# Six experts written out without a loop, and a reordered entry to the delta rule's triangular inverse

## The chip, the core and the metric

The kernel runs on one core of a Trainium2 chip: TensorE (matrix products, PE in the profile), VectorE (DVE), ScalarE (ACT), GpSimd (POOL) and SyncE (SP), which here issues the weight transfers. The engines run their own instruction streams and wait for each other on semaphores. The time is that of one execution on the device in microseconds, and the median over runs is what counts.

## The reference

The model is a trunk of two layers over 256 tokens of width 1024. The even layer adds a window attention with 8 heads (64 wide) and a gated delta rule with 4 heads (128 wide), followed by a dense SwiGLU. The odd layer is a Mamba-2 mixer, followed by a top-2-of-8 mixture of SwiGLU experts, 1024 by 3584 each. Each sub-layer ends in a layer norm of ALPHA * x + f(x). The two parts that the change touches are, in short:

```
# gated delta rule, per chunk and head
gc = cumsum(g);  decay = exp(gc_i - gc_j) below the diagonal
A  = strict_lower((beta k) k^T * decay);   attn = (q k^T) * decay
u, w = solve(I + A, [beta v, beta k exp(gc)])
v_new = u - w S;  o = (q exp(gc)) S + attn v_new
S = S exp(gc_last) + (k exp(gc_last - gc))^T v_new
# experts, all eight on the tokens that chose them
out += combine[:, e] * (silu(x Wg[e]) * (x Wu[e])) Wd[e]
```

## The kernel before

All weights come from HBM as fp32 in pieces of 1 MB into a ring of raw buffers. ScalarE rounds each piece into a high part (w_hi, L698 and L951), VectorE subtracts to get the low part (w_lo, L1127 and L1575), and TensorE multiplies three times: high by high, high by low, low by high (in the experts L2366 to L2368). Nothing schedules the work: each engine's stream stands in the source in the order in which it runs, with waits on semaphores that are written by hand. PSUM is one tensor `ps` of eight banks of 128x512 fp32. The delta rule's tiles all lie in one SBUF tensor, so the profile calls them "arena"; here they are told apart by their lines.

**Entry to the delta rule.** The 256 tokens make two row tiles t = 0, 1, and each row tile is one chunk of 128 for the four heads. TensorE runs the projections; the last is that of the attention's queries, `halves(N_Q, ...)`, in two halves, with `running_sums` between them (L1928, L1929): the running sums of g, into bank 3. VectorE, after the low part of the projection's last piece (L1127), normalises k and q (L1210, L1212), copies the attention's k and v (L1216), negates the running sums (L1218, L1219), copies the attention's queries (L1223) and applies the rotary tables. TensorE then spreads the running sums and beta over rows (L1943 to L1948) and forms the products k k^T and k q^T (`kk_products`, L1937 and L1938). ScalarE makes the decays (L760). VectorE multiplies products and decays into attnT (L1250) and AT (L1251, L1252). Then TensorE turns k and v (L1958), VectorE scales them into kdec, vb and kbe (L1256 to L1262), and the inverse starts.

**The inverse** has seven levels (LEVELS) for both row tiles. `level(lv)` masks AT into LT (L1271); TensorE multiplies LT by X (L2050); ScalarE copies the result (L796); TensorE multiplies by XT (L2060, L2061); VectorE subtracts (L1352, L1354 in level 0, L1357, L1359 later). Between the levels stand pieces of the window attention: `turn_qk` transposes its queries (L1969) and its key (L1973), VectorE copies them (L1279, L1281), and so on. The queries' transposes wait for the scalings of k and v (semaphore kv_scaled), since they reuse banks.

**The experts.** Expert 0 starts outside the loop. A loop `Fori(0, E - 2, 2)` on TensorE, ScalarE, VectorE and SyncE then runs three passes, each of which finishes expert i, runs expert i + 1 and begins expert i + 2 (`expert_rest`, `expert_head`); experts 6 and 7 end outside. Inside the loop the counts waited for are computed in registers. Near the end of each expert's steady part TensorE turns the next expert's tokens, eight transposes (L2362).

Of the kernel before, what the change touches and what calls it, by code (L numbers as in the profile page):

```python
# [35 lines left out]
P = 128  # L36
# [26 lines left out]
E = 8  # L63
# [112 lines left out]
def build(nc, dram, out, limit=99):  # L176
    with ExitStack() as ctx:
# [297 lines left out]
        def _(sp):  # L475
# [110 lines left out]
            with sp.Fori(0, E - 2, 2) as i:  # L586
                link_loads(i, (i, 0), i + 1)
                steady_loads(i + 1, (i, 1))
                link_loads(i + 1, (i, 1), i + 2)
                steady_loads(i + 2, (i, 2))  # L590
# [85 lines left out]
        def _(act):  # L676
# [80 lines left out]
            for t in range(TT):  # L757
                act.wait_ge(sem("dn_gcrow"), t + 1)
                for h in range(DH):
                    act.activation(decT[:, t * DH + h, :], ps[:, t, h * P:(h + 1) * P], ACT.Exp, bias=ngc[:, t, h:h + 1]  # L760
                                   ).then_inc(sem("dn_dec"), 1)

# [300 lines left out]
            with act.Fori(0, E - 2, 2) as i:  # L1063
                expert_rest((i, 0), 0, (i, 1), False, i + 1)
                expert_head((i, 1), 1, (i, 0), i)
                expert_rest((i, 1), 1, (i, 2), False, i + 2)
                expert_head((i, 2), 0, (i, 1), i + 1)
# [27 lines left out]
        def _(dve):  # L1095
# [109 lines left out]

            n = N0 - 1
            dense_low(n, n % RAW_D, n % CUT)
            rn3 = rn[:, :].rearrange("p (k t) -> p k t", t=SEQ)
# [4 lines left out]

            dve.wait_ge(d_piece_used, CUT + N_KV + 2)
            for t in range(TT):
                dve.tensor_copy(qkv[:, t, 512:768], ps[:, 4 + t, 0:256]).then_inc(sem("kv_copied"), 1)  # L1216
            dve.wait_ge(sem("dn_gc"), 1)
            link(TS(ngc[:, :, :], ps[:, 3, 0:TT * DH].rearrange("p (t h) -> p t h", t=TT), -1.0, None, ALU.mult))  # L1218
            TTO(ddk[:, :], ps[:, 3, 8:12], ngc[:, 0, :], ALU.add).then_inc(sem("dn_cols"), 1)  # L1219
# [25 lines left out]

            for t in range(TT):
                dve.wait_ge(sem("dn_dec"), DH * (t + 1))
                dve.wait_ge(sem("dn_kk"), t + 1)
                hs = slice(t * DH, (t + 1) * DH)
                TTO(attnT[:, hs, :], four(ps[:, 6 + t, :]), decT[:, hs, :], ALU.mult)  # L1250
                link(TTO(AT[:, hs, :], four(ps[:, 4 + t, :]), decT[:, hs, :], ALU.mult))  # L1251
                TTO(AT[:, hs, :], AT[:, hs, :], four(ps[:, 2 + t, :]), ALU.mult).then_inc(sem("dn_A"), 1)  # L1252
            dve.wait_ge(sem("dn_A"), TT)

            dve.wait_ge(sem("kv_turned"), 1)
            TTO(kdec[:, :, :], four(ps[:, 4, :]), bc(dke[:, :], P), ALU.mult)  # L1256
            dve.wait_ge(sem("kv_turned"), 2)
            TTO(vb[:, 0:4, :], four(ps[:, 5, :]), bc(beta[:, 0, :], P), ALU.mult)
            dve.wait_ge(sem("kv_turned"), 3)
            TTO(kbe[:, :, :], four(ps[:, 6, :]), bc(bege[:, :], P), ALU.mult)  # L1260
            dve.wait_ge(sem("kv_turned"), 4)
            TTO(vb[:, 4:8, :], four(ps[:, 7, :]), bc(beta[:, 1, :], P), ALU.mult).then_inc(sem("kv_scaled"), 1)  # L1262
# [82 lines left out]
            level(1)  # L1345
            for lv in range(LEVELS):
# [14 lines left out]
                if lv == 0:  # L1361
                    dve.wait_ge(sem("inv_X"), 2)
                if lv + 2 < LEVELS:
                    level(lv + 2)
# [378 lines left out]
            with dve.Fori(0, E - 2, 2) as i:  # L1743
                expert_rest((i, 0), 0, (i, 1), i, None, rank)
                expert_head((i, 1), 1, None, None)
                expert_rest((i, 1), 1, (i, 2), i + 1, None, rank)
                expert_head((i, 2), 0, None, None)
# [59 lines left out]
        def _(pe):  # L1807
# [115 lines left out]
            def running_sums():  # L1923
                pe.wait_ge(sem("dn_gb"), 1)
                pe.wait_ge(sem("norm_ln"), 4)
                pe.wait_ge(sem("ln_loaded"), 16 * 3)
                g8 = gdn[:, :, :].rearrange("p t h -> p (t h)")
                mm(ps[:, 3, 0:8], tri, g8, start=True, stop=True)  # L1928
                mm(ps[:, 3, 8:12], ones[:, :], gdn[:, 0, :], start=True, stop=True).then_inc(sem("dn_gc"), 1)  # L1929
# [11 lines left out]
            pe.wait_ge(sem("dn_cols"), 1)  # L1941
            for t in range(TT):
# [6 lines left out]
            pe.wait_ge(sem("dn_qk"), 2)  # L1949
            for t in range(TT):  # L1950
                pe.wait_ge(sem("q_copied"), t + 1)
                pe.wait_ge(sem("kv_copied"), t + 1)
                kk_products(t)
            pe.wait_ge(sem("dn_A"), TT)
            for t in range(TT):
                for w_ in range(2):
                    for h in range(DH):
                        last = pe.transpose(ps[:, 4 + 2 * t + w_, h * P:(h + 1) * P], dnT[:, 4 + 4 * w_ + h, t * P:(t + 1) * P], ident)  # L1958
                    last.then_inc(sem("kv_turned"), 1)

# [82 lines left out]
            for lv in range(LEVELS):  # L2043
                for t in range(TT):
# [6 lines left out]
                    last.then_inc(sem("inv_P"), 1)  # L2051
                attention(lv, 0)
# [434 lines left out]
            with pe.Fori(0, E - 2, 2) as i:  # L2487
# [43 lines left out]
```

## Time and profile before

| what | value |
|---|---|
| median of 3 runs | 1596.58 us (1596.31 to 1596.8) |
| profiled execution | 1595.24 us |
| its span, first to last instruction | 1593.4 us |
| TensorE busy | 1559.8 us, 98% |
| VectorE busy | 1280.6 us, 80% |
| ScalarE busy | 970.1 us, 61% |
| granted TensorE clock, mean | 0.996 of full speed |
| chain that ended last | TensorE 92%, VectorE 5% |

The profile is of one execution. Its span is measured from the first to the last instruction, and 1.84 us of the execution's time lie around it. Busy time is the sum of an engine's instructions; a share near 100% says that the time can fall only where that engine waits, or by giving it less to do. The chain that ended last is followed back from the last instruction to whatever released each step, so it shows what the end of the program hung on.

### The profile page before, as it was taken

What the parts mean: (1) busy time and instruction counts of PE and PEld (TensorE: products, weight loads), DVE (VectorE), ACT (ScalarE), POOL (GpSimd) and SP (SyncE); (2) the same over time, 40 slices, a digit from 0 to 9 for tenths busy, and PEclk for the clock granted to TensorE, in tenths of its full rate; (3) what the DMA queues carried; (4) which work ended last, traced back from release to release, by engine and by line L of the source; (5) the groups of instructions that cost most, each with busy time, mean ns of one, the idle gap of its engine ahead of it and who ended that gap; (6) DMA issues with size and microseconds to landing.
All of it is one profiled execution on the core that took longest, in us unless ns stands there. A gap on an engine that the chain in (4) does not pass through costs nothing.

```text
span 1593.4 us, 22120 instructions
## 1 busy us (share of the span) xinstructions
PE 1559.8 (98%) x8609; PEld 1324.1 (83%) x8609; DVE 1280.6 (80%) x1060; ACT 970.1 (61%) x822; POOL 55.1 (3%) x43
## 2 busy tenths in 40 slices
PE   9989999999999999999999999999999999999996
PEld 7878599997999787888888878888878888888885
DVE  6777645447777797999889889889889888888997
ACT  4414244443553644777777777777777777777773
POOL 4000000002000000020000000000000000000100
PEclk9999999999999999999999999999999999999998
DMA  9250365554557118999999999999999999999992
GB/s 323 70 196 1 114 203 184 184 185 156 179 177 261 62 35 307 360 399 395 394 394 383 387 378 363 389 380 377 384 379 370 383 374 378 392 372 389 394 397 79
DMA packets 221760, 459.40 MB, mean 288 GB/s; under 512 B 7685, under 2 KB 64737, under 8 KB 221665
## 3 DMA queue, kind: packets, MB, share of 16 engines
q1 hardware_dynamic: 215488, 441.76, 76.4%
q10 hardware_dynamic: 4464, 11.60, 2.0%
q0 software_dynamic: 1712, 4.68, 0.8%
q8 instruction: 70, 1.15, 0.3%
q14 instruction: 26, 0.21, 0.0%
HBM read 444.38 MB, written 13.63 MB: 287 GB/s over the span
## 4 chain that ended last, share of the span: by engine, by line
PE 92%; DVE 5%; ACT 1%; issue 1%; POOL 0%; DMA 0%; DVEq 0%; ACTq 0%
PE ps L2366 19%; PE ps L2368 19%; PE ps L2367 19%; PE ps L1849 6%; PE ps L1851 6%; PE ps L1850 6%; PE ps L1842 2%; PE ps L2391 2%; PE ps L2130 1%; PE ps L2131 1%; PE ps L2132 1%; PE ps L2291 1%; PE ps L2293 1%; PE ps L2292 1%; PE ps L2060 1%
## 5 line engine op out<-in xcount | busy, mean ns | idle before, releaser
L1575 DVE TENSOR_TENSOR w_lo<-raw,w_hi 128x2048 fp32r<-128x2048 f32 x252 | 576.8, 2291 | 69.2 <-ACT w_hi L951 68.3
L951 ACT CAST w_hi<-raw 128x2048 fp32r<-128x2048 f32 x252 | 482.8, 1916 | 129.2 <-PE ps L2368 129.2
L2366 PE MATMUL ps<-w_hi,xg_hi 128*128 128x512 f32 x672 | 267.7, 398 | 3.1 <-issue 2.3
L2368 PE MATMUL ps<-w_hi,xg_lo 128*128 128x512 f32 x672 | 262.4, 391 | 0.0
L2367 PE MATMUL ps<-w_lo,xg_hi 128*128 128x512 f32 x672 | 261.6, 389 | 0.0
L698 ACT CAST w_hi<-raw 128x2048 fp32r<-128x2048 f32 (+1 forms) x72 | 135.6, 1883 | 182.1 <-PE ps L1851 133.6
L1127 DVE TENSOR_TENSOR w_lo<-raw,w_hi 128x2048 fp32r<-128x2048 f32 (+1 forms) x71 | 167.7, 2367 | 94.7 <-ACT w_hi L698 94.7
L1849 PE MATMUL ps<-xT_hi,w_hi 128*128 128x256 f32 x768 | 218.1, 284 | 0.3 <-DVE xT_lo L1120 0.3
L1851 PE MATMUL ps<-xT_hi,w_lo 128*128 128x256 f32 x768 | 217.4, 283 | 0.0
L1850 PE MATMUL ps<-xT_lo,w_hi 128*128 128x256 f32 x768 | 217.4, 283 | 0.0
L1575 DVE TENSOR_TENSOR xT_lo<-raw,xT_hi 128x2048 fp32r<-128x2048 f32 x84 | 192.3, 2290 | 29.9 <-ACT xT_hi L951 29.9
L951 ACT CAST xT_hi<-raw 128x2048 fp32r<-128x2048 f32 x84 | 160.9, 1915 | 43.8 <-PE ps L2368 43.8
L2366 PEld LDWEIGHTS ps<-w_hi,xg_hi 128*128 128x128 f32 x672 | 126.3, 188 | 28.8 <-issue 4.0
L1849 PEld LDWEIGHTS ps<-xT_hi,w_hi 128*128 128x128 f32 x768 | 147.4, 192 | 1.7 <-DVE xT_lo L1120 1.3
L2368 PEld LDWEIGHTS ps<-w_hi,xg_lo 128*128 128x128 f32 x672 | 126.2, 188 | 27.2
L1850 PEld LDWEIGHTS ps<-xT_lo,w_hi 128*128 128x128 f32 x768 | 147.4, 192 | 0.3
L1851 PEld LDWEIGHTS ps<-xT_hi,w_lo 128*128 128x128 f32 x768 | 147.4, 192 | 0.0
L2367 PEld LDWEIGHTS ps<-w_lo,xg_hi 128*128 128x128 f32 x672 | 126.5, 188 | 24.6
L2366 PE MATMUL ps<-w_hi,ehT_hi 128*128 128x512 f32 x336 | 131.5, 391 | 0.0
L2367 PE MATMUL ps<-w_lo,ehT_hi 128*128 128x512 f32 x336 | 130.8, 389 | 0.0
L2368 PE MATMUL ps<-w_hi,ehT_lo 128*128 128x512 f32 x336 | 130.8, 389 | 0.0
L2368 PE MATMUL ps<-xT_hi,xg_lo 128*128 128x512 f32 x224 | 87.3, 390 | 0.0
(398 smaller groups left out, 2164.4 us busy)
## 6 DMA issues: line engine op xcount, KB each, us to landing
raw<-in_moe_w_gate SPq DMA_DIRECT2D x112, 1024.0 KB, 7.8
raw<-in_moe_w_up SPq DMA_DIRECT2D x112, 1024.0 KB, 8.4
raw<-in_moe_w_down SPq DMA_DIRECT2D x112, 1024.0 KB, 8.4
raw<-in_ssm_w_in SPq DMA_DIRECT2D x20, 1024.0 KB, 5.3
raw<-in_ffn_w_gate SPq DMA_DIRECT2D x11, 1024.0 KB, 5.3
raw<-in_ffn_w_up SPq DMA_DIRECT2D x11, 1024.0 KB, 5.3
raw<-in_ffn_w_down SPq DMA_DIRECT2D x11, 1024.0 KB, 4.9
raw<-in_even_w_in SPq DMA_DIRECT2D x10, 1024.0 KB, 12.9
```

The source lines that it names most:

```text
L698: act.copy(w_hi[:, c, 0:size], raw[:, i, 0:size]).then_inc(sem("dense_hi_made"), 1)
L951: act.copy(e_hi((n + 2 * odd) % CUT_E), raw[:, i, :]).then_inc(sem("hi_made"), 1)
L1127: TTO(w_lo[:, c, 0:size], raw[:, i, 0:size], w_hi[:, c, 0:size].bitcast(F32), ALU.subtract).then_inc(d_lo_made, 1)
L1575: TTO(e_lo(c), raw[:, n % RAW, :], e_hi(c).bitcast(F32), ALU.subtract).then_inc(lo_made, 1)
L1842: last = mm(ps[:, 4 + 2 * t + n, :], mixT[:, k, t * P:(t + 1) * P], w[:, kk, 512 * n:512 * n + 512], start=k == 0, stop=k == KD - 1)
L1849: mm(out_ap, whi, xT_hi[:, k, :], start=first, stop=False)
L1850: mm(out_ap, whi, xT_lo[:, k, :], start=False, stop=False)
L1851: return mm(out_ap, wlo, xT_hi[:, k, :], start=False, stop=last_)
L2366: mm(out_ap, hi, whi, start=start, stop=False)
L2367: mm(out_ap, hi, wlo, start=False, stop=False)
L2368: return mm(out_ap, lo, whi, start=False, stop=stop)
L2391: last = pe.transpose(ps[:, 4, c * P:(c + 1) * P], eh[:, side(j), c * P:(c + 1) * P], ident)
```

## The change

It has two parts that share no code.

First, the loop over pairs of experts becomes a Python loop on all four engines (the diff shows the line on ScalarE; SyncE, VectorE and TensorE have the same), which writes experts 1 to 6 out as straight code with constant counts. The order of the work inside is the same.

Second, the entry to the delta rule's inverse:
- The running sums go to bank 4 behind the attention's k and v (columns 256 to 267), and so wait for the copies of k and v in place of the logarithms of the norms. VectorE makes those copies ahead of the last low part, and negates the sums right behind it.
- TensorE interleaves the two row tiles: rows and products of tile 0, then of tile 1.
- attnT of tile 1 is made after level 0's masks (`made_attn`), and level 1's masks after level 0's differences.
- The transposes of k and v run by row tile (`turn_kv`): tile 0 ahead of the inverse, tile 1 behind level 0's product.
- ScalarE, in place of VectorE, scales them: 16 activations with a scale per partition, behind the decays.

```diff
-            with act.Fori(0, E - 2, 2) as i:
+            for i in range(0, E - 2, 2):
...
+            act.wait_ge(sem("dn_dke"), 2)
+            act.wait_ge(sem("dn_gb"), 1)
+            for i, (dst, by) in enumerate(((kdec[:, :, :], dke[:, :]), (vb[:, 0:4, :], beta[:, 0, :]),
+                                           (kbe[:, :, :], bege[:, :]), (vb[:, 4:8, :], beta[:, 1, :]))):
+                act.wait_ge(sem("kv_turned"), i + 1)
+                bank = ps[:, (4, 6, 5, 7)[i], :]
+                for h in range(DH):
+                    last = act.activation(dst[:, h, :], bank[:, h * P:(h + 1) * P], ACT.Copy, scale=by[:, h:h + 1])
+            last.then_inc(sem("kv_scaled"), 1)
...
+            dve.wait_ge(d_piece_used, CUT + N_KV + 2)
+            for t in range(TT):
+                dve.tensor_copy(qkv[:, t, 512:768], ps[:, 4 + t, 0:256]).then_inc(sem("kv_copied"), 1)
             n = N0 - 1
             dense_low(n, n % RAW_D, n % CUT)
+            dve.wait_ge(sem("dn_gc"), 1)
+            link(TS(ngc[:, :, :], ps[:, 4, 256:264].rearrange("p (t h) -> p t h", t=TT), -1.0, None, ALU.mult))
+            TTO(ddk[:, :], ps[:, 4, 264:268], ngc[:, 0, :], ALU.add).then_inc(sem("dn_cols"), 1)
...
+            def made_attn(t):
+                hs = slice(t * DH, (t + 1) * DH)
+                return TTO(attnT[:, hs, :], four(ps[:, 6 + t, :]), decT[:, hs, :], ALU.mult)
...
-                TTO(attnT[:, hs, :], four(ps[:, 6 + t, :]), decT[:, hs, :], ALU.mult)
+                if t == 0:
+                    made_attn(0)
...
-            TTO(kdec[:, :, :], four(ps[:, 4, :]), bc(dke[:, :], P), ALU.mult)
...
             level(0)
-            level(1)
+            made_attn(1).then_inc(sem("dn_A"), 1)
...
                 if lv == 0:
                     dve.wait_ge(sem("inv_X"), 2)
+                    level(1)
...
                 pe.wait_ge(sem("dn_gb"), 1)
-                pe.wait_ge(sem("norm_ln"), 4)
                 pe.wait_ge(sem("ln_loaded"), 16 * 3)
+                pe.wait_ge(sem("kv_copied"), TT)
...
-            pe.wait_ge(sem("dn_qk"), 2)
-            for t in range(TT):
+                if t == 0:
+                    pe.wait_ge(sem("dn_qk"), 2)
                 pe.wait_ge(sem("q_copied"), t + 1)
                 pe.wait_ge(sem("kv_copied"), t + 1)
                 kk_products(t)
-            pe.wait_ge(sem("dn_A"), TT)
-            for t in range(TT):
+
+            def turn_kv(t):
+                pe.wait_ge(sem("dn_A"), (1, 3)[t])
                 for w_ in range(2):
                     for h in range(DH):
-                        last = pe.transpose(ps[:, 4 + 2 * t + w_, h * P:(h + 1) * P], dnT[:, 4 + 4 * w_ + h, t * P:(t + 1) * P], ident)
+                        last = pe.transpose(ps[:, 4 + t + 2 * w_, h * P:(h + 1) * P], dnT[:, 4 + 4 * w_ + h, t * P:(t + 1) * P], ident)
                     last.then_inc(sem("kv_turned"), 1)
+
+            turn_kv(0)
...
                     last.then_inc(sem("inv_P"), 1)
+                if lv == 0:
+                    turn_kv(1)
```

VectorE's rows from the first product with the decays on, before (L1250 attnT, L1251 and L1252 AT, L1256 to L1262 the scalings, L1271 masks, L1352 and L1354 the differences of level 0):

```order
L1250 TENSOR_TENSOR arena<-ps,arena 128x512
L1251 TENSOR_TENSOR arena<-ps,arena 128x512
L1252 TENSOR_TENSOR arena<-arena,ps 128x512
L1250 TENSOR_TENSOR arena<-ps,arena 128x512
L1251 TENSOR_TENSOR arena<-ps,arena 128x512
L1252 TENSOR_TENSOR arena<-arena,ps 128x512
L1256 TENSOR_TENSOR arena<-ps,arena 128x512
L1258 TENSOR_TENSOR arena<-ps,arena 128x512
L1260 TENSOR_TENSOR arena<-ps,arena 128x512
L1262 TENSOR_TENSOR arena<-ps,arena 128x512
L1271 TENSOR_TENSOR arena<-arena,const 128x512 x4
```

and in the changed kernel, whose lines are others (L1256 attnT, L1264 and L1265 AT, L1275 masks, L1356 and L1358 the differences):

```order
L1256 TENSOR_TENSOR arena<-ps,arena 128x512
L1264 TENSOR_TENSOR arena<-ps,arena 128x512
L1265 TENSOR_TENSOR arena<-arena,ps 128x512
L1264 TENSOR_TENSOR arena<-ps,arena 128x512
L1265 TENSOR_TENSOR arena<-arena,ps 128x512
L1275 TENSOR_TENSOR arena<-arena,const 128x512 x2
L1256 TENSOR_TENSOR arena<-ps,arena 128x512
L1356 TENSOR_TENSOR arena<-const,arena 128x512
L1358 TENSOR_TENSOR arena<-const,ps 128x512
L1356 TENSOR_TENSOR arena<-const,arena 128x512
L1358 TENSOR_TENSOR arena<-const,ps 128x512
L1275 TENSOR_TENSOR arena<-arena,const 128x512 x4
```

The four scalings are gone, attnT of tile 1 stands behind the first two masks, and level 1's masks stand with those of level 2 behind the differences.

TensorE's rows behind the key products, before, with the semaphores waited for (L1958 transposes of k and v, L2050 the inverse's products, L1969 transposes of the queries):

```order
L1958 MATMUL ps<-const,arena 128x128 [waits dn_A]
L1958 MATMUL ps<-const,arena 128x128 x15
L2050 MATMUL ps<-const,arena 128x128 [waits inv_L]
L2050 MATMUL ps<-const,arena 128x128 x3
L2050 MATMUL ps<-const,arena 128x128 [waits inv_L]
L2050 MATMUL ps<-const,arena 128x128 x3
L1969 MATMUL ps<-const,arena 128x128 [waits kv_scaled,rope_done]
L1969 MATMUL ps<-const,arena 128x128 x7
L2050 MATMUL ps<-arena 128x128 [waits inv_X,inv_L]
L2050 MATMUL ps<-arena 128x128 x3
L2050 MATMUL ps<-arena 128x128 [waits inv_X,inv_L]
```

and in the changed kernel (L1965, L2059 and L1978 in the same roles):

```order
L1965 MATMUL ps<-const,arena 128x128 [waits dn_A]
L1965 MATMUL ps<-const,arena 128x128 x7
L2059 MATMUL ps<-const,arena 128x128 [waits inv_L]
L2059 MATMUL ps<-const,arena 128x128 x3
L2059 MATMUL ps<-const,arena 128x128 [waits inv_L]
L2059 MATMUL ps<-const,arena 128x128 x3
L1965 MATMUL ps<-const,arena 128x128 [waits dn_A]
L1965 MATMUL ps<-const,arena 128x128 x7
L1978 MATMUL ps<-const,arena 128x128 [waits kv_scaled,rope_done]
L1978 MATMUL ps<-const,arena 128x128 x7
L2059 MATMUL ps<-arena 128x128 [waits inv_X,inv_L]
```

The sixteen transposes are split in two eights, the second of which stands between the inverse's first product and the queries.

TensorE's rows where the loop over pairs begins, before (L2487 is the loop, L2366 to L2368 an expert's three products):

```order
L2368 MATMUL ps<-xT_hi,ehT_lo 128x512
L2487 UNCONDITIONAL_BRANCH
L2487 ISA
L2378 ISA [waits e_h]
L2366 MATMUL ps<-w_hi,xg_hi 128x512 [waits lo_made]
L2367 MATMUL ps<-w_lo,xg_hi 128x512
L2368 MATMUL ps<-w_hi,xg_lo 128x512
```

and at the same place in the changed kernel, where the products are L2377 to L2379:

```order
L2379 MATMUL ps<-xT_hi,ehT_lo 128x512
L2377 MATMUL ps<-w_hi,xg_hi 128x512 [waits lo_made,e_h]
L2378 MATMUL ps<-w_lo,xg_hi 128x512
L2379 MATMUL ps<-w_hi,xg_lo 128x512
L2377 MATMUL ps<-w_hi,xg_hi 128x512
```

The branch and the two register instructions are gone, and the wait for e_h stands on the product itself.

## Rows read from the trace of the kernel before

**Rows 1.** The page: busy time, share of span, instructions; queue: packets, MB, share.
```profile
PE 1559.8 (98%) x8609; PEld 1324.1 (83%) x8609; DVE 1280.6 (80%) x1060; ACT 970.1 (61%) x822; POOL 55.1 (3%) x43
...
q8 instruction: 70, 1.15, 0.3%
```

**Rows 2.** Chain that ended last, experts: start us, us, what; issue is unexplained time.
```profile
852.76 0.87 PE ps L2362 x8
943.08 1.19 issue
972.74 0.88 PE ps L2362 x8
1091.22 0.87 PE ps L2362 x8
1181.54 1.07 issue
1211.06 0.87 PE ps L2362 x8
1329.54 0.87 PE ps L2362 x8
1448.02 0.87 PE ps L2362 x8
```

**Rows 3.** Busy us of PE, PEld, DVE, ACT, POOL; clock, DMA, GB/s by stretch.
```profile
90.00:99.00 9.00, 4.73 (x41) 4.31 (x40) 8.15 (x14) 0.00 (x0) 0.00 (x0) 1.00 1.10 352
700.00:940.00 240.00, 240.00 (x1095) 198.86 (x1095) 213.54 (x119) 178.55 (x121) 0.00 (x0) 1.00 1.03 389
1580.00:1593.00 13.00, 1.20 (x6) 0.64 (x4) 10.44 (x17) 0.00 (x0) 2.09 (x2) 0.63 0.22 84
```

**Rows 4.** Timeline of TensorE, delta rule's entry: start us, us, operation, [idle before].
```profile
76.48 0.36 PE L1928 MATMUL ps<-arena,const 128*128 128x8 f32 x2 [1.01 <-issue]
...
76.92 0.48 PE L1880 MATMUL ps<-w_hi,xT_hi 128*128 128x512 f32 x1
...
82.49 0.39 PE L1943 MATMUL ps<-maskb,identb 128*128 128x512 bf16 x1
...
89.85 0.39 PE L1938 MATMUL ps<-arena 128*128 128x128 f32 x2
92.57 1.96 PE L1958 MATMUL ps<-const,arena 128*128 128x128 f32 x16 [2.34 <-DVE arena L1252]
96.47 2.05 PE L2050 MATMUL ps<-const,arena 128*128 128x128 f32 x16 [1.94 <-DVE arena L1271]
98.36 1.04 PE L1969 MATMUL ps<-const,arena 128*128 128x128 f32 x8
99.57 2.33 PE L2050 MATMUL ps<-arena 128*128 128x128 f32 x16 [0.17 <-DVE arena L1354]
102.61 0.44 PE L1973 MATMUL ps<-const,arena 128*128 128x128 f32 x2 [0.71 <-DVE arena L1279]
```

**Rows 5.** Timeline of VectorE in the same stretch.
```profile
74.10 2.29 DVE L1127 TENSOR_TENSOR w_lo<-raw,w_hi 128x2048 fp32r<-128x2048 f32 x1 [0.99 <-ACT w_hi L698]
...
81.16 0.75 DVE L1216 COPY arena<-ps 128x256 f32<-128x256 f32 x2
...
88.59 0.69 DVE L1250 TENSOR_TENSOR arena<-ps,arena 128x512 f32<-128x512 f32 x1 [2.82 <-PE ps L1938]
...
93.33 0.69 DVE L1256 TENSOR_TENSOR arena<-ps,arena 128x512 f32<-128x512 f32 x1 [0.82 <-PE ps L1958]
...
95.74 2.49 DVE L1271 TENSOR_TENSOR arena<-arena,const 128x512 f32<-128x512 f32 x4
```

**Rows 6.** Timeline of ScalarE, logarithms, exponentials of decays, one attention exponential.
```profile
73.97 2.41 ACT L750 ACTIVATE arena<-ps,eps_rms 128x512 f32<-128x512 f32 x4
...
83.81 1.14 ACT L760 ACTIVATE arena<-ps,arena 128x128 f32<-128x128 f32 x4 [1.30 <-PE ps L1945]
...
127.89 0.39 ACT L771 ACTIVATE arena<-arena 128x128 f32<-128x128 f32 x1
```

More of the change, by code:

```diff
@@ L585, in _ @@
             steady_loads(0, (0, 0))
-            with sp.Fori(0, E - 2, 2) as i:
+            for i in range(0, E - 2, 2):
                 link_loads(i, (i, 0), i + 1)
@@ L1062, in _ @@
             act.wait_ge(sem("x_placed"), 16 * 2 * TT)
-            with act.Fori(0, E - 2, 2) as i:
+            for i in range(0, E - 2, 2):
                 expert_rest((i, 0), 0, (i, 1), False, i + 1)
@@ L1212, in _ @@
             TTO(dnT[:, 4:8, :], dnT[:, 4:8, :], rn3[:, 4:8, :], ALU.mult).then_inc(sem("dn_qk"), 1)
-            dve.wait_ge(d_piece_used, CUT + N_KV + 2)
-            for t in range(TT):
[L1216 to L1219, printed above, removed]
             dve.wait_ge(d_piece_used, CUT + N0)
@@ L1253, in _ @@
             dve.wait_ge(sem("dn_A"), TT)
-            dve.wait_ge(sem("kv_turned"), 1)
-            TTO(kdec[:, :, :], four(ps[:, 4, :]), bc(dke[:, :], P), ALU.mult)
[L1257 to L1262, printed above, removed]
             def level(lv):
@@ L1742, in _ @@
             expert_head((0, 0), 0, None, None, False, True)
-            with dve.Fori(0, E - 2, 2) as i:
+            for i in range(0, E - 2, 2):
                 expert_rest((i, 0), 0, (i, 1), i, None, rank)
@@ L1924, in running_sums @@
                 pe.wait_ge(sem("dn_gb"), 1)
-                pe.wait_ge(sem("norm_ln"), 4)
                 pe.wait_ge(sem("ln_loaded"), 16 * 3)
+                pe.wait_ge(sem("kv_copied"), TT)
                 g8 = gdn[:, :, :].rearrange("p t h -> p (t h)")
-                mm(ps[:, 3, 0:8], tri, g8, start=True, stop=True)
-                mm(ps[:, 3, 8:12], ones[:, :], gdn[:, 0, :], start=True, stop=True).then_inc(sem("dn_gc"), 1)
+                mm(ps[:, 4, 256:264], tri, g8, start=True, stop=True)
+                mm(ps[:, 4, 264:268], ones[:, :], gdn[:, 0, :], start=True, stop=True).then_inc(sem("dn_gc"), 1)
             pe.wait_ge(sem("dn_conv"), NDN // 2)
@@ L1941, in _ @@
             pe.wait_ge(sem("dn_cols"), 1)
+            pe.wait_ge(sem("norm_ln"), 4)
             for t in range(TT):
@@ L1953, in _ @@
                 kk_products(t)
-            pe.wait_ge(sem("dn_A"), TT)
-            for t in range(TT):
+            def turn_kv(t):
+                pe.wait_ge(sem("dn_A"), (1, 3)[t])
                 for w_ in range(2):
                     for h in range(DH):
-                        last = pe.transpose(ps[:, 4 + 2 * t + w_, h * P:(h + 1) * P], dnT[:, 4 + 4 * w_ + h, t * P:(t + 1) * P], ident)
+                        last = pe.transpose(ps[:, 4 + t + 2 * w_, h * P:(h + 1) * P], dnT[:, 4 + 4 * w_ + h, t * P:(t + 1) * P], ident)
                     last.then_inc(sem("kv_turned"), 1)
+            turn_kv(0)
             def turn_qk(n):
@@ L2486, in _ @@
             expert_head((0, 0), 0, None, 0)
-            with pe.Fori(0, E - 2, 2) as i:
+            for i in range(0, E - 2, 2):
                 expert_rest((i, 0), 0, (i, 1), False, True)
```

## The prediction

> **What bounds the kernel now.** I read the page first: TensorE is busy 98% of the span [rows 1]. So a change is worth what it takes out of TensorE's idle time, and nothing else. Then the chain of waits, to see where that idle time lies near the edits. In the experts the reader is to look for the eight-transpose rows of L2362, which come once per expert. From 972.74 to 1091.22 and from 1329.54 to 1448.02 they stand 118.48 us apart, but from 852.76 to 972.74 it is 119.98 and from 1091.22 to 1211.06 it is 119.84 [rows 2]. In each of the two long stretches lies one "issue" row (1.19 and 1.07 us), time in which TensorE waited for nothing that the profile shows, and each is where the loop over pairs jumps back. There are three passes, so two jumps. The way out of the loop, which is no jump, lies between 1329.54 and 1448.02 and costs nothing. Inside a pass TensorE is never idle: 240.00 of 240 us [rows 3].
>
> Last the timelines of the delta rule. TensorE stands still four times: 1.01 us before the running sums, 2.34 before the k and v transposes (L1958), 1.94 before the inverse's first products (L2050), 0.71 before L1973 [rows 4]. The last three wait for VectorE, which works there without a pause. So around 88 to 102 us VectorE's queue sets the end.
>
> **The experts written out.** It removes the two jumps back on TensorE, and those of ScalarE, VectorE and SyncE, whose own delay at the same places lies behind TensorE's. What goes is (119.98 - 118.48) + (119.84 - 118.48) = 1.50 + 1.36 = 2.86 us. If only the visible idle time goes, it is 1.19 + 1.07 = 2.26; I take 2.86, since the straight stretches show the whole period without a jump. Arithmetic on registers goes too, at no gain, since the periods inside a pass already have TensorE full. SyncE's transfers keep their order and their waits. What is added is code that is read once instead of a body read three times; the trace of before shows no written-out run of experts 1 to 6, so the lower bound is a loss, priced below as a rival.
>
> A rule of the Trainium skill bears on this (Runtime: NRT & Kernel Launch, section "Instruction fetch mechanics"): code is fetched ahead in sequence only, and a taken branch to a page that isn't held stalls the engine. By that rule both jumps go and the sum stays 2.86. The same section says that crossing a block is "mostly hidden", which leaves open what the written-out code pays; that is the rival.
>
> **The delta rule's entry, step by step**, with times on the clock of the trace of before.
>
> 1. The running sums no longer wait for the logarithms (L750, which end at 73.97 + 2.41 = 76.38 [rows 6]). They run at 75.47, right behind the first half of the queries' projection. But its second half also needs the low part of its weights, which VectorE makes from 74.10 to 76.39 [rows 5]. So it starts at about 76.47 in place of 76.92: 0.45 us, not 1.01. The two copies of k and v (0.75 us) now stand ahead of that low part; VectorE was idle 0.99 us there, so they are covered with 0.24 to spare. Were they not, the whole chain would slip by what is missing.
> 2. From 82.49 TensorE runs back to back for 7.58 us, until 89.85 + 0.22 [rows 4]; the edit only interleaves the two row tiles. It now starts at 82.04, tile 0 is done after half of it, at 85.83, tile 1 at 89.62. VectorE's three products of a tile take 1.97 us (88.59 to 92.52, two tiles [rows 4, 5]). Those of tile 0 are now hidden under TensorE's tile 1. Behind tile 1 stand two products in place of three, about 1.4 us: done at 91.15 in place of 92.52.
> 3. The four scalings (from 93.33 to 95.74, 2.41 us) leave VectorE, and level 1's mask goes behind. So level 0's two masks (0.6 us each, from four in 2.4) run from 91.2, and the inverse's first product starts at 92.0 in place of 96.47. It takes 1.89 us for both tiles, to 93.9. The second half of the k and v transposes (eight, 0.9 us) follows to 94.8; the first half ran at 89.6 to 90.5, while TensorE waited anyway.
> 4. A new wait: the query transposes need all four scalings, now on ScalarE. It was idle there, with nothing queued behind but the copies of the next level. The trace has no such scaling. The nearest row is four exponentials of the same 128x128 tiles from PSUM: 1.14 us [rows 6]. The first two sets run at 90.2 to 92.5, hidden. The last two can start at 94.4 and take 2.28, to 96.7. From above, one by one at 0.39, which one activation of this size takes alone [rows 6], they take 3.12, 0.8 us later. From below, at no cost, the wait vanishes and level 1's mask (96.2) becomes the late one, 1.4 us better. I take 1.14 a set, the same tile shape.
> 5. The query transposes start at 96.8 (before 98.36), 0.9 us for two tiles. Level 1's product starts at 97.7 (99.57). By then VectorE has finished four differences (93.0 to 95.5) and four masks (to 98.0), and copies the first turned tile by 98.7. So level 1's product ends at 99.6 and the key transpose follows at once, where it was waiting for that copy until 102.61. It takes 0.22, not the 0.44 after a wait. The next products begin at 99.85 in place of 103.05.
>
> That is 3.2 us on the path (2.4 to 4.6 by the bounds of step 4). Behind it every engine has the same order as before, and nothing waits for a fixed time: each later start shifts alike.
>
> **Sum.** 2.86 + 3.2 = 6.1 us. The profiled execution took 1595.24 us (span 1593.4 and 1.84 around it), which gives 1589.1. The median of the runs, 1596.58, lies 1.34 above the profiled one; on its scale the forecast is 1590.5.
>
> **Rivals.**
> - *Only the experts gain.* The scalings' wait takes the place of the removed one: the query transposes start as late as before and 3.2 us stay. For this the last two scalings would have to take more than twice 2.28 us and hold back the pass up to the key transpose. The idle ScalarE and the exponentials' row speak against it. Time 1596.6 - 2.9 = 1593.7.
> - *Only the delta rule gains.* Two or three new stalls of the jump's size in the written-out code eat the 2.86. Time 1596.6 - 3.2 = 1593.4.
> - *Slower: TensorE runs out of code.* The larger instruction queue moved 70 packets; TensorE has 8609 matmul records [rows 1], each with a weight load (a pass shows 1095 and 1095 in 240 us [rows 3]), so 246 records a packet. A pass is nine packets; three passes are 27 places where the next packet could come late behind weight transfers, which move 389 GB/s there. A late one costs what a jump does, 1.13 us on average. From six such stalls the gain is gone; if one place in three stalls, the time is 1590.5 + 9 x 1.13 = 1600.7. Against it: the loop's passes, longer than anything else in the experts, show 240.00 us of work in 240. That packet count fits all executed records, so the body seems to be read anew in each pass already, without a stall within. The rule named above, with crossings mostly hidden, says the same.
> - *Neither shows.* 1596.6. A clock that fell in the delta rule would do this: the granted clock was 0.63 of 2.4 GHz in the last 13 us, between its two levels, after TensorE had nearly stopped (1.20 us of work). But with 4.73 us of work in the 9 us from 90 it stayed at 1.00 [rows 3], and the new order leaves shorter pauses, about 1.5 and 2.0 us.
>
> **How the numbers follow.** Forecast 0.72, only experts 0.08, only delta rule 0.10, neither 0.04, slower 0.06. The likeliest case alone spans 4.7 (2.26 + 2.4) to 7.5 (2.86 + 4.6): 1589.1 to 1591.9. The two half cases end at 1593.7, so the range that should hold 8 in 10 is 1589.0 to 1593.8. A measurement of this kernel can tell about 0.2% (3.2 us) from no change. Only-delta sits on that line and is split: faster 0.72 + 0.05 = 0.77, same 0.08 + 0.05 + 0.04 = 0.17, slower 0.06.
>
> **What would show it.** Right: all L2362 periods 118.48, and no "issue" row between them; the second half of the queries' projection at 76.5; the inverse's first product at 92.0, about 4.5 earlier; the query transposes released by ScalarE at about 96.8 after a pause of some 2 us; and everything from the key products to the output projection 3.2 earlier. Wrong: issue gaps of TensorE inside an expert, a lower granted clock after 90 us, VectorE's low part later than 76.4, or a pause of TensorE later in the inverse that was not there before.

## The result, and the profile after

| | before | changed |
|---|---|---|
| median of 6 runs, us | 1596.69 (1595.88 to 1597.97) | 1589.75 (1588.71 to 1591.40) |
| profiled execution, us (span) | 1595.24 (1593.4) | 1589.78 (1588.0) |

The ratio is 0.9949 [0.9939, 0.9959]: 8.1 us faster [6.5, 9.7] on 1596.58, which makes 1588.4. That is 0.6 us below the lower edge of the forecast's range, and a gain 2.0 us larger than the 6.1 forecast. The ratio is not the quotient of the two medians in the table; that is 0.9957, or 6.9 us. The same kernel run again (`after_again`, below) gave 6.5 us by its ratio and 8.5 by its medians. So the gain is known only to within 6.5 to 8.5 us; all four figures lie above the 6.1 forecast, and the two smaller ones would have lain inside its range. The two profiled executions differ by 5.46 us, 0.6 less than forecast. So the trace shows less gain than the timed runs, and that gap is the thing to explain.

First the page of the changed kernel; these two rows answer to [rows 1].

```profile
PE 1557.5 (98%) x8608; PEld 1323.1 (83%) x8609; DVE 1277.9 (80%) x1056; ACT 975.7 (61%) x838; POOL 55.1 (3%) x43
...
q8 instruction: 64, 1.05, 0.3%
```

The chain that ended last, in the experts, as in [rows 2] (L2362 is now L2373): start us, us, what.

```profile
850.21 0.87 PE ps L2373 x8
968.69 0.87 PE ps L2373 x8
1087.17 0.88 PE ps L2373 x8
...
1205.65 0.87 PE ps L2373 x8
...
1442.61 0.87 PE ps L2373 x8
```

All periods are 118.48, and no "issue" row stands between. One window over all the experts (busy us of PE, PEld, DVE, ACT, POOL; clock, DMA, GB/s) answers to the 240 us of [rows 3]: TensorE has 920.00 us of work in 920.

```profile
640.00:1560.00 920.00, 920.00 (x4193) 762.22 (x4193) 824.54 (x473) 687.28 (x466) 17.70 (x8) 1.00 1.02 383
```

The timeline of TensorE in the delta rule's entry, which answers to [rows 4]:

```profile
75.53 0.29 PE L1933 MATMUL ps<-arena,const 128*128 128x8 f32 x2
...
76.66 0.50 PE L1885 MATMUL ps<-w_hi,xT_hi 128*128 128x512 f32 x1 [0.62 <-DVE w_lo L1136]
...
92.26 2.05 PE L2059 MATMUL ps<-const,arena 128*128 128x128 f32 x16 [1.43 <-DVE arena L1275]
...
97.11 1.06 PE L1978 MATMUL ps<-const,arena 128*128 128x128 f32 x8 [1.93 <-ACT arena L769]
98.01 1.95 PE L2059 MATMUL ps<-arena 128*128 128x128 f32 x16
99.80 0.38 PE L1982 MATMUL ps<-const,arena 128*128 128x128 f32 x2
100.02 0.39 PE L2071 MATMUL ps<-arena 128*128 128x128 f32 x2
```

The pauses that were 1.01, 2.34, 1.94 and 0.71 us are now 0.62, 1.43 and 1.93. The new wait is the one forecast, L1978 for ScalarE. ScalarE's two pairs of scalings (compare [rows 6]) take 2.18 us each, where 2.28 was taken from the exponentials:

```profile
90.52 2.18 ACT L769 ACTIVATE arena<-ps,arena 128x128 f32<-128x128 f32 x8 [2.06 <-PE ps L1965]
94.79 2.18 ACT L769 ACTIVATE arena<-ps,arena 128x128 f32<-128x128 f32 x8 [2.09 <-PE ps L1965]
```

Where the 5.46 us of the two traces came from is read off where the same instruction stands in both. At the start the changed kernel loses 0.21: its first product with weights starts at 11.19 in place of 10.98, in code that no edit touches. The first product behind the key transposes (L2071) is this one in the kernel before:

```profile
102.88 0.39 PE L2060 MATMUL ps<-arena 128*128 128x128 f32 x2
```

It now starts 2.87 earlier, so the entry gave 3.08. Mamba's output projection at about 575 us gives 0.3 back; the loop adds 2.86; 5.4 in all.

### The profile page after: what moved, and what is told of

Its sections match the earlier page's. It is cut to its first block, busy times and chain, and to the rows that moved or that the text cites. A ratio compares the mean times of both kernels' runs of the same rounds, so it can differ in the third digit from the quotient of the medians.

```text
span 1588.0 us, 20779 instructions
## 1 busy us (share of the span) xinstructions
PE 1557.5 (98%) x8608; PEld 1323.1 (83%) x8609; DVE 1277.9 (80%) x1056; ACT 975.7 (61%) x838; POOL 55.1 (3%) x43
## 4 chain that ended last, share of the span: by engine, by line
PE 92%; DVE 5%; ACT 1%; issue 1%; POOL 0%; DMA 0%; DVEq 0%; SPq 0%; ACTq 0%
PE ps L2377 19%; PE ps L2379 19%; PE ps L2378 19%; PE ps L1854 6%; PE ps L1856 6%; PE ps L1855 6%; PE ps L1847 2%; PE ps L2402 2%; PE ps L2142 1%; PE ps L2141 1%; PE ps L2143 1%; PE ps L2302 1%; PE ps L2303 1%; PE ps L2304 1%; PE ps L2059 1%
## 5 line engine op out<-in xcount | busy, mean ns | idle before, releaser
L2377 PE MATMUL ps<-w_hi,xg_hi 128*128 128x512 f32 x672 | 267.3, 398 | 0.8 <-DVE w_lo L1580 0.5
L2379 PE MATMUL ps<-w_hi,xg_lo 128*128 128x512 f32 x672 | 262.3, 390 | 0.0
L2379 PEld LDWEIGHTS ps<-w_hi,xg_lo 128*128 128x128 f32 x672 | 126.1, 188 | 27.3
L2377 PEld LDWEIGHTS ps<-w_hi,xg_hi 128*128 128x128 f32 x672 | 126.3, 188 | 25.8 <-issue 0.9
L2377 PE MATMUL ps<-w_hi,ehT_hi 128*128 128x512 f32 x336 | 131.4, 391 | 0.0
L2379 PE MATMUL ps<-w_hi,ehT_lo 128*128 128x512 f32 x336 | 130.7, 389 | 0.0
L2379 PE MATMUL ps<-xT_hi,xg_lo 128*128 128x512 f32 x224 | 87.2, 389 | 0.0
```

The costliest lines, as they stand in the source:

```text
L2377: mm(out_ap, hi, whi, start=start, stop=False)
L2379: return mm(out_ap, lo, whi, start=False, stop=stop)
```

## The experiments

The theory was that of the forecast: two jumps of TensorE's loop, and a chain in the entry that is 3.2 us shorter. The rivals: the extra gain in the timed runs comes from the other engines' jumps, from the entry, or from a jump whose price is not fixed. A time "of before" below is a median of runs on the same chip, beside the kernel in question.

### The changed kernel again, and its two parts alone

`after_again` is the changed kernel itself. `loop_only` is the kernel before with the four loops written out:

```diff
-            with pe.Fori(0, E - 2, 2) as i:
+            for i in range(0, E - 2, 2):
```

`delta_only` is the changed kernel with the four loops put back (the same lines, turned round).

> The changed kernel, run again for its size. Theory one (the two profiles tell the size): about 5.5 to 6 us under the kernel before, ratio 0.9963. Theory two (an execution without the profiler gains more than the profiled one): about 8 us, ratio 0.995. In its profile either theory expects seven expert periods of 118.48 us and an inverse that starts some 4.2 us earlier.

> The kernel before with only the experts written out. Theory one: 2.9 us less, ratio 0.9982. Theory two, if the jumps cost more outside the profiled execution: 4 to 5 us less, ratio 0.997. Rival (the two parts need each other, or the written-out code stalls): no change. In the profile the two long expert periods, 119.98 and 119.84, should read 118.48.

> The changed kernel with the loop over pairs put back: only the delta rule's entry is changed. Theory one: 2.6 to 3.1 us less, ratio 0.9982. Theory two, if the extra gain lies here: 5 us less, ratio 0.997. The sum of this and of the experts written out alone should give the whole change, if the parts are independent. In the profile two expert periods should again be 1.4 us longer than the others.

| | median us | ratio to before |
|---|---|---|
| before | 1598.46 (1595.01 to 1601.73, 21 runs) | |
| after_again | 1589.94 (1589.66 to 1593.22, 6) | 0.9959 [0.9946, 0.9971] |
| loop_only | 1592.60 (1592.26 to 1593.74, 8) | 0.9970 [0.9960, 0.9980] |
| delta_only | 1596.49 (1593.48 to 1599.43, 12) | 0.9988 [0.9978, 0.9998] |

Both parts gain. Writing the experts out is worth 1598.46 - 1592.60 = 5.9 by the medians and 4.8 [3.2, 6.4] by the ratio, which is theory two of that run and more than the 2.86 forecast. The entry is worth 1592.60 - 1589.94 = 2.7 by the medians and 1.9 [0.3, 3.5] by the ratio of `delta_only`. The two ratios together make 6.7, about the whole change (6.5 by the ratio of `after_again`), so the parts look independent. `after_again` itself decides nothing: the ratios of both its theories (0.9963 and 0.995) lie inside its interval. The spread speaks too, though the counts of runs differ: 6 to 7 us with the loop, 1.5 to 3.6 without.

The profile of `delta_only` shows why. Its chain in the experts:

```profile
852.01 0.87 PE ps L2373 x8
...
942.33 1.10 issue
...
971.90 0.87 PE ps L2373 x8
...
1090.38 0.87 PE ps L2373 x8
...
1212.92 0.87 PE ps L2373 x8
```

The first jump costs 119.89 - 118.48 = 1.41, as in the kernel before. The second costs 122.54 - 118.48 = 4.06. TensorE's timeline there, and a window (columns as above), say what the rest is:

```profile
1182.87 0.49 PE L2377 MATMUL ps<-w_hi,xg_hi 128*128 128x512 f32 x1 [2.18 <-DVE w_lo L1580]
...
1184.17 0.63 PE L2378 MATMUL ps<-w_lo,xg_hi 128*128 128x512 f32 x1
1184.60 0.63 PE L2379 MATMUL ps<-w_hi,xg_lo 128*128 128x512 f32 x1
...
1187.31 0.39 PE L2377 MATMUL ps<-w_hi,xg_hi 128*128 128x512 f32 x1
1187.54 0.39 PE L2378 MATMUL ps<-w_lo,xg_hi 128*128 128x512 f32 x1
```

```profile
1184.00:1186.00 2.00, 2.00 (x6) 1.54 (x6) 0.95 (x1) 0.00 (x0) 0.00 (x0) 0.50 1.04 396
```

The pause was 2.18 us long, and behind it the granted clock stood at 0.50, which is 1.2 of 2.4 GHz: products start 0.43 us apart instead of 0.23, for some eight products. So 2.18 us of the 4.06 are the pause and about 1.6 (eight times 0.20) the clock. The remaining 0.3 stands at the first jump too, whose pause of 1.10 cost 1.41.

### Whose jump it is

`pe_straight` is the kernel before with TensorE's loop alone written out; `others_straight` has the other three engines' loops written out and TensorE's kept.

```diff
-            with pe.Fori(0, E - 2, 2) as i:       # pe_straight
+            for i in range(0, E - 2, 2):
...
-            with act.Fori(0, E - 2, 2) as i:      # others_straight; dve and sp alike
+            for i in range(0, E - 2, 2):
```

> The kernel before with only TensorE's stream written out; ScalarE, VectorE and SyncE keep their loops. If TensorE's own jump is what costs, the whole 2.9 us go, as with all four written out. If the jumps of ScalarE or VectorE hold TensorE up, the long periods stay and the gain is under 1 us.

> The kernel before with ScalarE, VectorE and SyncE written out and TensorE's loop kept. If TensorE's own jump back is the whole cost (theory A), nothing is gained: the median stays at some 1597 to 1598 us, single runs spread over 4 us or more as in the kernel before, and two expert periods of the profile are 1.3 to 4 us longer than 118.48. If the other engines' jumps matter (rival), the long periods shrink.

`pe_straight`: 1592.40 (1591.86 to 1593.86, 6 runs), ratio 0.9969 [0.9957, 0.9981], all periods 118.48: the whole gain of `loop_only`. `others_straight`: 1597.52 (1594.79 to 1600.91, 12 runs) beside 1597.23 of before, ratio 0.9996 [0.9985, 1.0006], its jumps 1.32 and 4.12 us (the second period runs from 1091.17 to 1213.77): no gain. So the cost is TensorE's own jump, and the forecast was right that the others' lie behind it.

The profile can mislead here. At the second jump of `others_straight`, TensorE's row names VectorE as the releaser; below it VectorE's row that ends in that pause:

```profile
1183.70 0.49 PE L2366 MATMUL ps<-w_hi,xg_hi 128*128 128x512 f32 x1 [2.22 <-DVE w_lo L1575]
```

```profile
1180.80 2.29 DVE L1575 TENSOR_TENSOR w_lo<-raw,w_hi 128x2048 fp32r<-128x2048 f32 x1 [0.35 <-ACT w_hi L951]
```

That low part ends at 1183.09, 91.92 us behind the eight transposes at 1091.17. In the changed kernel the same low part also ends 91.92 behind its transposes (850.21):

```profile
939.84 2.29 DVE L1580 TENSOR_TENSOR w_lo<-raw,w_hi 128x2048 fp32r<-128x2048 f32 x1 [0.35 <-ACT w_hi L960]
```

There TensorE passes the place without any wait; its product starts 1.77 us before that low part is done, so it does not need it:

```profile
940.36 0.39 PE L2377 MATMUL ps<-w_hi,xg_hi 128*128 128x512 f32 x1
```

So VectorE was not late; its semaphore merely was the last to move during the pause.

### How far, and how many

`one_jump` is the changed kernel with a loop over experts 1 to 4 and 5 and 6 written out, so one jump stays. `near_jump` writes the experts out as the changed kernel does, but runs steps 2 to 5 of each of experts 0 to 6 on TensorE as a loop of two passes with two steps each, a jump back over 152 products and their weight loads. The jump of the kernel before goes back over some 1080 (1095 is the count of the 240 us of [rows 3]; a pass takes 236.96 us):

```diff
-                for j in range(1, HEAD_STEPS + 1):
+                for j in range(1, 2 if near else HEAD_STEPS + 1):
...
+                with pe.Fori(0, 2, 1) as p:
+                    for jj in (2, 3):
```

> The changed kernel with a loop of two passes and the third pair written out: one jump back in place of two or none. Theory A (each far jump costs 1.4 us or, in some executions, 3 to 4, because a pause of 2 us can be followed by a lower clock): half of the way between the changed kernel and the one with the loop put back, some 1592 to 1593.5 us, with a spread between theirs. Rival (the first entry of a loop or its register arithmetic costs): nearly the whole way, 1595 or more.

> The changed kernel with a short loop on TensorE alone: in each of experts 0 to 6 the steps 2 to 5 run as two passes of two steps, seven jumps back over some 150 matmuls in place of jumps over 1095. Theory A (the jump costs because the code that it goes to is no longer held): no stall at these jumps, periods of 118.48 us and the changed kernel's 1590 us. Rival (any jump back costs in this traffic): at least 7 x 1.1 = 8 us more, 1598 us, and periods of 119.6 or more.

`one_jump`: 1593.74 (1591.97 to 1597.89, 11 runs), ratio 0.9974 [0.9962, 0.9986]. That is just above theory A's 1592 to 1593.5 and below the rival's 1595. One period is long, 1.78 us over:

```profile
851.88 0.87 PE ps L2388 x8
...
942.20 1.47 issue
...
972.14 0.87 PE ps L2388 x8
```

`near_jump`: 1589.88 (1588.83 to 1591.69, 6 runs), ratio 0.9950 [0.9934, 0.9966], the changed kernel's time. It jumps seven times, and every period is 118.48, the first from here:

```profile
852.00 0.87 PE ps L2373 x8
...
970.48 0.87 PE ps L2373 x8
```

So a jump as such, with its register arithmetic, costs nothing here; the far one does. The medians make the one jump of `one_jump` dearer than its profile, 3.9 us above `near_jump`. In that profile 1.6 us more are lost in the entry, where the clock fell (below).

Whether the code is read again can be seen on the larger instruction queue, first of `one_jump`, then of `near_jump`:

```profile
q8 instruction: 67, 1.10, 0.3%
```

```profile
q8 instruction: 56, 0.92, 0.2%
```

All four profiles with two far jumps of TensorE have 70 packets, `others_straight` among them, `one_jump` has 67, and those without a jump have 64 or 65, `pe_straight` among them. So this queue follows TensorE's loop and no other's, and the far jump brings two or three packets more than straight code. The short loops bring eight fewer. At 2 x 8609 records in the 64 packets of the changed kernel, 269 each, the 7 x 304 records that are run a second time would fill eight packets. So the code of the short loop was not read again, and that of the long one was.

By the Trainium skill (Runtime: NRT & Kernel Launch, section "Instruction fetch mechanics") a taken branch stalls the engine if its target isn't in the current two-page window, and TensorE's instruction memory has room for 2048 instructions. The runs agree: the 304 of the short loop cost nothing, the some 2160 of the long one did. The page gives no price.

### The jump's price in another execution

> The kernel before, profiled once more, to see its two jumps in another execution. Theory A (a jump's cost varies between executions): the two long periods of the eight-transpose rows differ from 119.98 and 119.84; at least one is 120.3 or more, up to 122.6 with the granted clock below 1.00 behind it. Rival B (it is fixed, and the executions of the loop kernels that cost 122.5 owe it to their other edits): 119.8 to 120.0 twice, the profiled time 1595.0 to 1595.6.

The kernel before, profiled once more, took 1595.91 us. Its chain:

```profile
852.85 0.87 PE ps L2362 x8
...
973.29 0.87 PE ps L2362 x8
...
1091.77 0.87 PE ps L2362 x8
...
1211.74 0.87 PE ps L2362 x8
```

That is 120.44 and 119.97: 1.96 and 1.49 us. The same kernel had 1.50 and 1.36 in the trace that the forecast used. Over the five profiles with a far jump there are nine: 1.50, 1.36, 1.96, 1.49, 1.41, 4.06, 1.32, 4.12, 1.78, on average 2.11. So the price varies, as theory A had it; but the two dear ones stand in kernels with other edits, and the four of the kernel before itself reach 1.96 at most. Two jumps at the average of all nine are 4.2, 1.36 more than the 2.86 of the one trace; and the median of the runs lay 1.34 above that trace.

### The entry, edit by edit

`sums_wait` and `scale_dve` each undo one edit of the changed kernel.

```diff
+                pe.wait_ge(sem("norm_ln"), 4)          # sums_wait
...
-                    last = act.activation(dst[:, h, :], bank[:, h * P:(h + 1) * P], ACT.Copy, scale=by[:, h:h + 1])
...
+                return TTO(dst, four(ps[:, bank, :]), bc(by, P), ALU.mult)    # scale_dve: on VectorE
...
+            scale_kv(0)                    # behind level 0's masks
+            scale_kv(1)
...
+                    scale_kv(2)            # behind level 0's differences
+                    scale_kv(3).then_inc(sem("kv_scaled"), 1)
```

> The changed kernel with one edit undone: the running sums wait for the logarithms of the norms again. By step 1 of the forecast the second half of the queries' projection starts at 77.1 in place of 76.66, all behind it 0.4 us later, the inverse's first product at 92.7 in place of 92.26, span 1588.4. Rival: VectorE's negation of the sums stands behind its last low part in any case, so nothing behind the key products moves: first product at 92.3, span 1588.0.

> The changed kernel with the four scalings of k and v back on VectorE, two behind level 0's masks and two behind level 0's differences; bank and interleaving as in the changed kernel. Each set is 0.60 to 0.69 us on VectorE. Theory A (VectorE's queue was the bound, the move to ScalarE carries a good part of the 3 us): the inverse's first product still starts at 92.3, but level 0's differences and the last scalings end about 1.3 us later than before the edit, so the query transposes start at 97.5 to 98.5 in place of 97.11 and the next products 1.0 to 1.5 us later than 99.80, span 1589.0 to 1589.5. Rival B (splitting the transposes by tile and reordering the masks is the whole gain, ScalarE's part is hidden anyway): next products at 99.8 within 0.3, span 1588.0 to 1588.3.

In `sums_wait` TensorE's first sixteen transposes took 3.68 us against 2.20, and all behind them began some 2 us late (why is open). So times are read against the end of the projection's first half, whose last product starts at 77.26 (75.30 in the changed kernel):

```profile
77.26 0.39 PE L1887 MATMUL ps<-w_hi,xT_lo 128*128 128x512 f32 x1
...
79.09 0.48 PE L1885 MATMUL ps<-w_hi,xT_hi 128*128 128x512 f32 x1
...
94.71 2.05 PE L2060 MATMUL ps<-const,arena 128*128 128x128 f32 x16 [1.43 <-DVE arena L1275]
```

The second half starts 1.83 us behind it, against 1.36: 0.47 later. The inverse's first product keeps that (17.45 behind it against 16.96). In this one profile the edit is worth what was forecast (0.45), and its rival falls. The time, 1591.05, carries the late start.

`scale_dve` took 1592.42 us. The first product stands at 92.32, but:

```profile
98.53 1.83 PE L1979 MATMUL ps<-const,arena 128*128 128x128 f32 x8 [3.28 <-DVE arena L1343]
...
102.86 0.38 PE L1983 MATMUL ps<-const,arena 128*128 128x128 f32 x2
```

```profile
98.00:100.00 2.00, 1.47 (x8) 1.50 (x9) 2.00 (x4) 0.00 (x0) 0.00 (x0) 0.66 1.10 350
100.00:102.00 2.00, 2.00 (x11) 2.00 (x10) 1.99 (x4) 0.00 (x0) 0.00 (x0) 0.50 0.67 210
```

The query transposes are 1.42 us later, as expected (98.53 beside 97.5 to 98.5). The key transposes, where the next products begin, are 3.06 later (102.86 against 99.80): behind the pause of 3.28 us the granted clock stood at 0.50, which is 1.2 GHz, and the eight transposes took 1.83 us against 1.06. That second part was not expected, and the 1592.42 of this single run carry it.

### Filling the pauses, and shortening them

`warm_entry` adds products that nobody reads to the two pauses; `early_queries` lets each half of the query transposes wait only for the set of scalings that frees its bank.

```diff
+            keep_running(2, 6)                          # warm_entry, behind turn_kv(0)
+                    keep_running(2, 8)                  # behind turn_kv(1)
...
-                    pe.wait_ge(sem("kv_scaled"), 1)     # early_queries
+                if n < TT:
+                    pe.wait_ge(sem("kv_scaled"), 2 + n)
```

(In `early_queries` each of ScalarE's four sets signals for itself, tile 1's values are turned and scaled ahead of its keys, and level 0's attention copy stands ahead of the later masks.)

> The changed kernel with 14 small extra bf16 products of TensorE laid into its two pauses in the delta rule's entry (6 behind tile 0's transposes, 8 behind tile 1's), whose results nobody reads. It asks whether these pauses sometimes bring the lower granted clock seen at 98 to 102 us in two other kernels' profiles, and with it the 3 us by which some executions of the changed kernel lie higher. Theory A (the pauses set it): the median is that of the changed kernel, 1589.8 within 0.5, but no execution lies above 1591, and the granted clock at 96 to 104 us is 1.00. Theory B (the high executions come from elsewhere, the stretch at 575 us for instance): the spread stays 1588.7 to 1593. Rival C: the extra products stand in the way of the inverse's, whose first product or query transposes start 0.3 to 1 us later, median 1590.1 to 1590.8.

> The changed kernel, where each query transpose waits only for the scaling that empties its own bank (the second k, v tile is turned and scaled v first), and VectorE copies the turned queries ahead of level 2's masks. If the wait for all four scalings is what is late, as forecast (1.93 us of pause in the profile), the key products start 1.2 to 1.6 us earlier: 1588.6 us, ratio 0.9991 to the changed kernel. If the masks of level 1 or the copies are late right behind it, under 0.5 us.

`early_queries`: 1588.13 (1587.35 to 1588.52, 5 runs), ratio 0.9939 [0.9922, 0.9956]. The wait of 1.93 is 0.36:

```profile
95.36 0.60 PE L1982 MATMUL ps<-const,arena 128*128 128x128 f32 x4
96.33 0.66 PE L1982 MATMUL ps<-const,arena 128*128 128x128 f32 x4 [0.36 <-ACT arena L769]
...
98.81 0.38 PE L1986 MATMUL ps<-const,arena 128*128 128x128 f32 x2
```

The key transposes start 0.99 us ahead of the changed kernel's (98.81 beside 99.80), although the inverse's first product starts 0.34 later (92.60 beside 92.26). That is 1.33 gained behind it, within the 1.2 to 1.6 expected, so that wait was on the path. Its experts' rows stand 1.41 ahead; the other 0.42 arose in the Mamba output projection. By its median it beats both kernels, but its interval overlaps with that of `near_jump`, which has the changed kernel's time.

`warm_entry`: 1588.83 (1588.63 to 1590.07, 5 runs), ratio 0.9949 [0.9935, 0.9962]. The extra products delay nothing: the query transposes start at 97.22, 0.11 later, as do the products ahead of both pauses. No run lies above 1591, where three of the changed kernel's twelve do; but at three in twelve, five runs without one come up about one time in four. The median is lower than the 1589.3 to 1590.3 of theory A. And its profile is 0.11 later at 97 us and 1.02 earlier at the experts, so its gain arose between, in the output projection of Mamba. There the clock differs from execution to execution. Below stand the changed kernel (1.00 again from 578 us on), then `warm_entry`, then `near_jump`, which had 0.56 at 574 to 578 us and 0.58 behind it. Its profiled run was one of the long ones (1591.56):

```profile
574.00:578.00 4.00, 3.51 (x10) 2.44 (x9) 4.00 (x3) 1.90 (x1) 2.59 (x1) 0.57 0.00 0
```

```profile
574.00:578.00 4.00, 3.37 (x15) 2.44 (x15) 4.00 (x3) 1.91 (x1) 2.68 (x1) 1.00 0.00 0
```

```profile
578.00:582.00 4.00, 4.00 (x12) 3.13 (x11) 4.00 (x7) 0.00 (x0) 0.00 (x0) 0.58 0.00 0
```

So the one long execution that was profiled owes its length to this stretch and not to the entry. Whether filling the entry's pauses helps anything stays open.

## Why the prediction was right or wrong

**The loop's mechanism** was right: TensorE's jump alone (`pe_straight`, `others_straight`), no stall in the written-out code, no cost of the way out. The rival "TensorE runs out of code" falls: 920.00 us of work in 920. The forecast's reading that the loop's body is read anew in each pass holds too: 70 packets with the loop, 64 written out, 56 where short loops save eight.

**The loop's size** is the step that failed: "1.50 + 1.36 = 2.86 us. If only the visible idle time goes, it is 1.19 + 1.07 = 2.26". Both bounds came from the same two jumps of one execution, so they bounded how a row is read, not how a jump varies. The runs put 1.3 to 4.1 us for a jump in its place: 4.2 for two by the nine profiled, 4.8 [3.2, 6.4] by `loop_only`'s ratio and 5.9 by its medians. That the medians lie above the nine profiled jumps is open.

**The sum** repeated the error: "The median of the runs, 1596.58, lies 1.34 above the profiled one; on its scale the forecast is 1590.5". The offset was carried over as if it belonged to every execution. But it fits what the jumps cost more on average than in that trace (4.2 - 2.86 = 1.36), and goes with them: the changed kernel's median lies 0.03 below its profiled time. With 4.2 for the jumps and 3.1 for the entry the same sum gives 1589.3, inside the measured 1588.4 [1586.8, 1590.0]. That nine jumps explain the offset is a fit of sizes; no run separates it, and it rests on the two dear jumps, neither of them in the kernel before. How far the sum missed is loose as well: 8.1 us was measured first and 6.5 again by the ratios, where 6.1 was forecast.

**The entry**, with 0.21 us of late start taken off the changed trace:

| step | forecast | trace |
|---|---|---|
| 1. second half of the queries' projection | 76.47 | 76.45 |
| 3. inverse's first product | 92.0 | 92.05 |
| 4. query transposes, released by ScalarE | 96.8 | 96.90 |
| 5. products behind the key transposes | 99.85 | 99.81 |

All four are within 0.1 us. The gain of 3.2 was 3.08 there, because those products began at 102.88 and not 103.05. One reading of the rows was not exact: VectorE, said to work "there without a pause", waits 0.82 us for the transposes of k and v in [rows 5]. What came out at the end is less than forecast: 2.7 by the medians and 1.9 [0.3, 3.5] by the ratio. Between them lies the Mamba output projection, where "each later start shifts alike" did not hold. There TensorE now waits 0.49 us for a low part until 575.22, a wait that the kernel before does not have, and the stretch of lower clock lies elsewhere (0.57 at 574 to 578 us); 0.3 us went back. Which of the two took it was not separated. Undoing step 1 or step 4 alone costs 0.47 and 1.42 us, the latter without the clock.

**The clock** was named under "Neither shows" and given little chance (0.04), since pauses got shorter. In the changed kernel's two profiles it stayed at 1.00 in the entry. In `delta_only` and `one_jump`, with the same entry and the same pause of about 1.9 us, it fell behind it (0.53 and 0.50 at 98 to 100 us), and 1.6 us of the entry's gain were gone in `delta_only`'s profile (the sixteen products behind it took 3.4 us in place of 1.8). First `after_again`, then `delta_only`:

```profile
98.00:100.00 2.00, 2.00 (x20) 2.00 (x19) 1.68 (x3) 0.58 (x1) 0.00 (x0) 1.00 1.10 350
```

```profile
98.00:100.00 2.00, 2.00 (x13) 2.00 (x11) 1.71 (x3) 0.00 (x0) 0.00 (x0) 0.53 1.10 348
```

So that rival exists at the entry, in some executions; why in these and not in others is open. The pause does not tell them apart: in `after_again` and `one_jump` TensorE's query transposes start at the same 97.25 behind the same pause of 1.92. Both kernels with the lower clock have a far jump in the experts, some 850 us later, and the four profiles with this pause and a clock of 1.00 (`after`, `after_again`, `near_jump`, `sums_wait`) have none; whether that is more than chance, two profiles can't tell.

**Only the experts, only the delta rule**: both fall by `loop_only` and `delta_only`, though the entry's part shows only just beside the loop's spread (0.9988 [0.9978, 0.9998]).

## What to carry to other kernels

A stall read from one profiled execution is one draw: before its size goes into a sum, read it in every occurrence and compare the spread of the timed runs, and ask whether the distance between the profile and the median is the very cost that the change removes. In this kernel a hardware loop over some 1080 products paid at each jump back of TensorE, and one over 152 was free; where between them the cost begins was not measured. When a row names an engine as the releaser, check whether the named work ends later than it does where there is no wait.

## What the runs showed of the hardware

- The price of a far jump on TensorE, with weight transfers running at some 380 GB/s, was 1.3 to 4.1 us over nine; a near one showed none in seven.
- The far jump's code was read again and the near one's was not: 70 packets on the instruction queue with two far jumps, 67 with one, 64 or 65 with none, 56 with seven near ones.
- The upper end of the price is not the fetch alone: behind the two pauses of about 2.2 us the granted clock stood at 1.2 GHz and cost another 1.6 or so; at the other seven jumps, with pauses of 1.0 to 1.7 us, it stayed at 2.4 GHz.
- Behind the same pause of 1.9 us in the same code the granted clock was 1.00 in three profiles (`after`, `after_again`, `near_jump`) and 0.50 or 0.53 in two (`one_jump`, `delta_only`).
- ScalarE's scaling of a 128x128 tile from PSUM with a factor per partition took 2.18 us for eight, close to the exponentials' 2.28.
